# Memory attention's scores as two products of fp32r parts, and a readiness of its own for each pair of heads

## The chip, the core and the metric

The kernel runs on one NeuronCore of a Trainium2 chip. The metric is the device time of one execution in microseconds (us), as the median of several runs. The engines are named as the profile names them: PE is TensorE (PEld is its weight load), DVE is VectorE, ACT is ScalarE, POOL is GpSimd and SP issues the loads from HBM. Each engine works through its own queue in order and waits on semaphores that the others raise.

## What is computed

The program is a small transformer: two layers with differential and forgetting attention over 528 tokens, then a second block over 512 tokens: a gated feed-forward, sparse and stick-breaking attention, cross attention to a memory of 256 tokens, and a last feed-forward. The change touches the cross attention alone:

```python
MEM_HEADS, HEAD_DIM, MEM_LEN = 4, 64, 256

def memory_cross_attention(h, mem_n, wq, wk, wv, wo, g_q, g_k):
    q = rms_norm((h @ wq).reshape(B, T, MEM_HEADS, HEAD_DIM), g_q)      # T = 512
    k = rms_norm((mem_n @ wk).reshape(B, M, MEM_HEADS, HEAD_DIM), g_k)  # M = 256
    v = (mem_n @ wv).reshape(B, M, MEM_HEADS, HEAD_DIM)
    s = jnp.einsum('bqhd,bkhd->bhqk', q, k).astype(jnp.float32) * HEAD_DIM ** -0.5
    p = jax.nn.softmax(s, axis=-1)
    o = jnp.einsum('bhqk,bkhd->bqhd', p, v).reshape(B, T, MEM_HEADS * HEAD_DIM)
    return o @ wo
```

## The kernel before

Activations lie transposed: features on the 128 partitions, tokens along the free dimension. A projection multiplies a weight chunk of 128x1024 with the activations, and both are kept as an fp32r high part and an fp32r low part; three products of parts stand for one product in fp32 (`mm3`, lines 470 to 472). For every weight chunk ACT makes the high part (line 446, `split_hi`) and POOL the low part (line 454, `split_lo`) in the order of the chunks.

The memory stage is written out engine by engine in `memory_pe`, `memory_act`, `memory_dve` and `memory_pool`; the order of each engine's work is the order of these lines, nothing is scheduled at run time. Its parts:

- "mk" 0 and 1 are the keys of the memory, "mq" 0 and 1 the queries, each a tile of 128 features: two heads of 64 features, on partitions 0 to 63 and 64 to 127. "mv" are the values, in two halves of the contraction, and "mo" the output projection. `wout2` is the projection of the stage before.
- A tile of keys or queries goes through `head_out_dve` (line 2149: PSUM times the norm's scale, into `xb`), `head_square_act` (line 2156), `head_norm_pe` (line 2162: mean of squares by a product), `head_norm_act` (lines 2168 and 2170: Ln and Exp) and `head_norm_dve` (line 2182: `xb` times gain and scale, in place).
- Then DVE copies the result for the scores: keys to `KM` (line 2869), queries to `QM` (line 2879). `QM` has one slot of 128 partitions for each of the 4 heads. A head fills 64 of its slot's partitions, the other 64 hold zeros, which a memset at the start of the stage writes (line 2845), so that a product over 128 partitions with `KM`, where both heads of a tile lie, gives one head's scores.
- The scores are 16 units (4 blocks of 128 queries by 4 heads): one fp32 product of 128x128 by 128x256 each. All wait for the copies of all four tiles: `ready=[(v_out, ("mk", 1, "put")), (v_out, ("mq", 1, "put"))]`.

`attention_pe`, `attention_act` and `attention_dve` walk through the units in steps. In step s PE transposes the probabilities of unit s-1 (line 1082), makes the scores of unit s+2 (line 1066), and multiplies the transposed probabilities of unit s-2 with the values (line 1097); three units are scored ahead of the first transposes. DVE takes the maximum of a unit's scores (line 1143), ACT the exponential with its sum (line 1122), and ACT or DVE copies the transposes out of PSUM (lines 1130 and 1159). DVE's first maximum stands behind the last copy to `QM` in its queue. The output projection follows (`mo_cols`).

`xb_read` guards a buffer: "mq" 1 goes to the same half of `xb` in which the keys lie, so it waits until they have been copied.

The sparse attention (`nsa_plan`, earlier in the program) already scores with fp32r parts. Its copies to high parts (line 2227, ACT) and subtractions to low parts (line 2219, DVE) write to `QN` and `KSW`.

Of the kernel before, what the change touches and what calls it, by code (L numbers as in the profile page):

```python
# [8 lines left out]
F32 = mybir.dt.float32  # L9
# [7 lines left out]
T = 512  # L17
# [134 lines left out]
def program(nc, wstream, wpairs, xT, memT, pos, const, param, out):  # L152
# [5 lines left out]
    with ctx:  # L158
# [128 lines left out]
        ml = sb("ml", [128, KT, 256], F32R, at=mem)  # L287
        KM = sb("KM", [128, 2, 256], at=mem)
        VM = sb("VM", [128, 2, 256], at=mem)
        QM = sb("QM", [128, 4, T], at=mem)  # L290
        Pb3 = sb("Pb3", [128, 4, L], at=mem)
# [1834 lines left out]
        def xb_read(on, key):  # L2126

            if key == ("mq", 1):
                on.wait_ge(*v_out["mk", 1, "put"])
            elif key in NORMED[2:]:  # L2130
                was = NORMED[NORMED.index(key) - 2]
                on.wait_ge(*roped[was + ("cos",)])
                on.wait_ge(*rot[was])
# [619 lines left out]
        def memory_pe(e, on):  # L2753
# [41 lines left out]
            for m in range(3, KT):  # L2795
                claim(on, pair(("mo", m), SINGLES), 1, v_out["mo", m])
                mo_cols(m, 0, T, 3).then_inc(*(rows("mo", m) if m % 4 < 3 else tile("mo", m // 4)))

        def mo_done(m):
            return rows["mo", m] if m % 4 < 3 else tile["mo", m // 4]  # L2800

        def memory_act(e, on):
# [18 lines left out]
            head_norm_act(e, on, ("mk", 0))  # L2821
            head_norm_act(e, on, ("mk", 1))
            split_hi(e, on, PART["mq", 1] + 2)
            head_norm_act(e, on, ("mq", 0))
            head_square_act(e, on, ("mq", 1), [sums["memx", 0, 0]])
            split_hi(e, on, PART["mv", 0, 0] + 2)
            head_norm_act(e, on, ("mq", 1))
            for i in range(2):
                on.wait_ge(*token_done("mv", 0, i, 2))
                on.wait_ge(*v_one["rt", "memkv"])  # L2830
                e.activation(VM[:, i, :], token_out("mv", 0, i, 256), ACT.Copy, scale=rTm[:, i:i + 1]).then_inc(
                    *a_out("mv", 0, i))
# [10 lines left out]
        def memory_dve(e, on):  # L2843
            on.wait_ge(*pv["sb", 7])
            e.memset(QM[:, :, :], 0.0).then_inc(*v_one("qm"))
            for c in range(KT):
# [19 lines left out]
            for c in range(2):  # L2866
                head_norm_dve(e, on, ("mk", c))
                on.wait_ge(*x_norm["mk", c])
                e.tensor_copy(KM[:, c, :], head_cols(("mk", c))[1]).then_inc(*v_out("mk", c, "put"))
            head_out_dve(e, on, ("mq", 1), rst[:, 0:T])  # L2870
            for c in range(2):
                head_norm_dve(e, on, ("mq", c))
                if c == 0:
                    turned_scale_dve(e, on, "memkv", 2, rTm)
                on.wait_ge(*x_norm["mq", c])
                on.wait_ge(*v_one["qm"])
                src = head_cols(("mq", c))[1]
                for j in range(2):
                    r = e.tensor_copy(QM[64 * j:64 * j + 64, 2 * c + j, :], src[64 * j:64 * j + 64, :])
                r.then_inc(*v_out("mq", c, "put"))  # L2880
            attention_dve(e, on, plans["mem"])
# [18 lines left out]
        def mem_plan():  # L2900
            units = []
            for i in range(4):
# [3 lines left out]
                for m in range(4):  # L2906
                    u = len(units)
                    units.append(Unit(
                        terms=[(QM[:, m, c0:c0 + 128], KM[:, m // 2, :], 0, 256, True, True)], n=256, o0=0,
                        banks=(u % 3, 1), ready=[(v_out, ("mk", 1, "put")), (v_out, ("mq", 1, "put"))],  # L2910
                        total=(rs[:, i % 2, m:m + 1], [(v_end, ("mem", i - 2, "recip"))] if i >= 2 else []), group=key,
# [350 lines left out]
```

## Time and profile before

| | before |
|---|---|
| median of 3 runs | 1870.87 us (1869.71 to 1872.06) |
| the profiled execution's own time | 1871.18 us |
| its span in the trace | 1869.4 us |
| granted TensorE clock, mean over the span | 0.999 of full speed |
| PE busy | 1831.7 us (98%) |
| DVE, ACT, POOL busy | 1152.4, 770.4, 466.5 us |

The trace shows for each instruction when it started on its engine, how long it took, and, where the engine stood idle ahead of it, for how long and what ended that. PE's matmuls are pipelined: neighbours overlap in the trace, so the distance between starts is their price, not the duration. Times in the rows are microseconds from the start of the span. The memory stage's keys, queries and values lie at about 1449 to 1477 us, its attention at 1477 to 1496 us.

### The profile page before, as it was taken

The page shows a single profiled execution, that of the slowest core. Times are in us where ns is not written, and L with a number is a line of the kernel's source. Part 1 is how long each engine was busy: PE and PEld are TensorE (multiplying, and loading weights), DVE is VectorE, ACT ScalarE, POOL GpSimd, SP SyncE. Part 2 cuts the span into 40 slices and gives each one's busy share as a digit, 9 for nine tenths or more (in the row PEclk, how much of TensorE's full clock was granted, in tenths as well). Part 3 has the DMA queues.
Part 4 walks back from the last instruction along what each step waited for, and adds up shares of the span by engine and source line. Part 5 has one row for each costly group of instructions (what it writes and reads, how often), then busy time and mean ns, then how long its engine had stood idle before and what let it go on. Part 6 is the DMA issues. An engine that isn't in the chain of part 4 may idle for free.

```text
span 1869.4 us, 29612 instructions
## 1 busy us (share of the span) xinstructions
PE 1831.7 (98%) x12020; PEld 1631.1 (87%) x12020; DVE 1152.4 (62%) x1677; ACT 770.4 (41%) x1392; POOL 466.5 (25%) x322
## 2 busy tenths in 40 slices
PE   8999999999999999999999999999999999999999
PEld 8999888979988887899988877989768878999887
DVE  7533465555416657999984555646556579999631
ACT  4122455311235644444433324445564644444331
POOL 5443211354341122000034423320003420000343
PEclk9999999999999999999999999999999999999999
DMA  4322000222220012432322223200003213323132
GB/s 165 97 84 91 35 12 13 80 90 103 80 90 2 23 46 80 140 109 91 102 74 94 98 102 126 86 24 1 1 1 120 84 57 126 115 99 103 69 100 102
DMA packets 41048, 145.49 MB, mean 78 GB/s; under 512 B 5072, under 2 KB 5328, under 8 KB 40784
## 3 DMA queue, kind: packets, MB, share of 16 engines
q1 hardware_dynamic: 40912, 143.59, 22.5%
q8 instruction: 96, 1.57, 0.3%
q14 instruction: 40, 0.33, 0.1%
HBM read 140.40 MB, written 2.10 MB: 76 GB/s over the span
## 4 chain that ended last, share of the span: by engine, by line
PE 87%; DVE 7%; ACT 3%; issue 2%; DMA 1%; POOL 0%; SPq 0%; DVEq 0%; ACTq 0%
PE ps L470 22%; PE ps L471 22%; PE ps L472 22%; PE ps L1066 6%; PE ps L1097 5%; PE ps L1082 2%; PE ps L2675 1%; PE ps L2658 1%; ACT wh L446 1%; DVE xl L560 1%; DVE XSl L1691 1%; PE ps L2416 1%; PE ps L2646 1%; PE ps L1276 1%; DMA raw<-wstream 1%
## 5 line engine op out<-in xcount | busy, mean ns | idle before, releaser
L454 POOL TENSOR_TENSOR wl<-raw,wh 128x1024 fp32r<-128x1024 f32 (+1 forms) x170 | 411.7, 2422 | 1032.8 <-ACT wh L446 1032.7
L446 ACT ACTIVATE wh<-raw 128x1024 fp32r<-128x1024 f32 (+1 forms) x178 | 188.5, 1060 | 604.7 <-PE ps L472 533.1
L470 PE MATMUL ps<-xh,wh 128*128 128x264 f32 (+3 forms) x1144 | 384.4, 336 | 9.5 <-DVE wl L466 3.4
L471 PE MATMUL ps<-xl,wh 128*128 128x264 f32 (+3 forms) x1144 | 380.8, 333 | 0.0
L472 PE MATMUL ps<-xh,wl 128*128 128x264 f32 (+3 forms) x1144 | 380.3, 332 | 0.0
L470 PE MATMUL ps<-XSh,wh 128*128 128x256 f32 (+1 forms) x864 | 284.2, 329 | 5.7 <-DVE wl L1749 3.7
L471 PE MATMUL ps<-XSl,wh 128*128 128x256 f32 (+1 forms) x864 | 284.1, 329 | 0.0
L472 PE MATMUL ps<-XSh,wl 128*128 128x256 f32 (+1 forms) x864 | 283.6, 328 | 0.0
L470 PEld LDWEIGHTS ps<-xh,wh 128*128 128x128 f32 x1144 | 215.2, 188 | 37.6 <-issue 7.3
L471 PEld LDWEIGHTS ps<-xl,wh 128*128 128x128 f32 x1144 | 215.3, 188 | 22.4 <-issue 1.0
L472 PEld LDWEIGHTS ps<-xh,wl 128*128 128x128 f32 x1144 | 215.4, 188 | 21.9
L470 PEld LDWEIGHTS ps<-XSh,wh 128*128 128x128 f32 x864 | 162.7, 188 | 23.5 <-issue 4.9
L472 PEld LDWEIGHTS ps<-XSh,wl 128*128 128x128 f32 x864 | 163.3, 189 | 15.9
L471 PEld LDWEIGHTS ps<-XSl,wh 128*128 128x128 f32 x864 | 162.8, 188 | 16.1
L470 PE MATMUL ps<-XSh,whx 128*128 128x256 f32 x496 | 139.9, 282 | 0.0
L471 PE MATMUL ps<-XSl,whx 128*128 128x256 f32 x496 | 139.7, 282 | 0.0
L472 PE MATMUL ps<-XSh,wlx 128*128 128x256 f32 x496 | 139.2, 281 | 0.0
L1143 DVE TENSOR_REDUCE nm<-ps 128x1 f32<-128x144 f32 (+7 forms) x208 | 100.0, 490 | 55.6 <-PE ps L1066 55.3
L470 PE MATMUL ps<-wh,xh 128*128 128x256 f32 (+1 forms) x352 | 100.6, 286 | 0.3 <-DVE xb L2149 0.3
L471 PE MATMUL ps<-wl,xh 128*128 128x256 f32 (+1 forms) x352 | 99.3, 282 | 0.0
L472 PE MATMUL ps<-wh,xl 128*128 128x256 f32 (+1 forms) x352 | 99.3, 282 | 0.0
L472 PEld LDWEIGHTS ps<-XSh,wlx 128*128 128x128 f32 x496 | 93.9, 189 | 0.0
(419 smaller groups left out, 3470.1 us busy)
## 6 DMA issues: line engine op xcount, KB each, us to landing
raw<-wstream SPq DMA_DIRECT2D x176, 512.0 KB, 3.3
rawx<-wpairs SPq DMA_DIRECT2D x44, 512.0 KB, 3.5
raw<-wpairs SPq DMA_DIRECT2D x24, 512.0 KB, 3.5
raw<-wstream SPq DMA_DIRECT2D x10, 528.0 KB, 3.4
h<-xT SPq DMA_DIRECT2D x4, 528.0 KB, 6.2
out<-h SPq DMA_DIRECT2D x8, 256.0 KB, 4.3
xs<-wpairs SPq DMA_DIRECT2D x2, 512.0 KB, 4.5
HF<-wpairs SPq DMA_DIRECT2D x2, 512.0 KB, 5.4
```

The costliest lines, as they stand in the source:

```text
L446: e.activation(wh[p % 2][:, 0:n], raw[c % 2][:, 0:n], ACT.Copy).then_inc(*w_hi(p))
L454: e.tensor_tensor(wl[p % 2][:, 0:n], raw[c % 2][:, 0:n], wh[p % 2][:, 0:n].bitcast(F32), ALU.subtract).then_inc(*w_lo(p))
L470: e.matmul(o, w_h, x_h, start=start, stop=False)
L471: e.matmul(o, w_h, x_l, start=False, stop=False)
L472: return e.matmul(o, w_l, x_h, start=False, stop=stop)
L560: e.scalar_tensor_tensor(dl, src, gain, dh.bitcast(F32), ALU.mult, ALU.subtract).then_inc(*v_lo(st, k))
L1066: r = e.matmul(ps[:, x.o0 + lo:x.o0 + hi], lhsT, rhs, start=start, stop=stop)
L1082: r = e.transpose(ps[0:b - a, 128 * j:128 * j + 128], plan.source(u)[:, a:b], ident)
L1097: r = e.matmul(PS[:, lo + x.cols[0]:lo + x.cols[1]], buf[0:b - a, 128 * j:128 * j + 128], x.value(j, b - a), start=j == 0 and (x.first or ...
L1143: e.tensor_reduce(nm[:, u % 8:u % 8 + 1], PS[:, lo:lo + x.n], AX.X, ALU.max, negate=True).then_inc(*peak(name, u))
L1276: r = e.transpose(ps[:, 128 * j:128 * j + nq], src[:, 128 * j:128 * j + 128], ident[0:nq, 0:nq])
L1691: e.tensor_tensor(mixed_rows(XSl, i), MIXED[i], mixed_rows(XSh, i).bitcast(F32), ALU.subtract).then_inc(*v_lo(st, "x", i))
```

## The change

`QM`, `KM` and a new `KML` hold fp32r. `QM` of a head now holds the query's high part on the head's own 64 partitions and its low part on the other 64; no zeros are left, and the memset goes. `KM` has a slot for each head, with the key's high part on both halves of the partitions; `KML` holds the key's low part once. A unit's scores are two products: `QM` by `KM` over 128 partitions (high by high and low by high), and the query's high half by `KML` over 64 partitions (high by low).

The high parts are made by ACT (`memory_high_act`: four copies of 64x256 for a key tile, two of 64x512 for a query tile), the low parts by DVE (`memory_low_dve`: two subtractions for a tile), which waits for ACT's. They replace DVE's copies. Units 0 and 1 wait for the parts of the keys and of "mq" 0, units 2 and 3 for those of "mq" 1.

```diff
-        KM = sb("KM", [128, 2, 256], at=mem)
+        KM = sb("KM", [128, 4, 256], F32R, at=mem)
+        KML = sb("KML", [128, 2, 256], F32R, at=mem)
-        QM = sb("QM", [128, 4, T], at=mem)
+        QM = sb("QM", [128, 4, T], F32R, at=mem)
...
             if key == ("mq", 1):
-                on.wait_ge(*v_out["mk", 1, "put"])
+                on.wait_ge(*v_lo["mk", 1])
...
+        def memory_high_act(e, on, key):
+
+            kind, c = key
+            on.wait_ge(*x_norm[key])
+            for j, (p0, p1) in enumerate(((0, 64), (64, 128))):
+                src = head_cols(key)[1][p0:p1]
+                if kind == "mq":
+                    r = e.activation(QM[p0:p1, 2 * c + j, :], src, ACT.Copy)
+                else:
+                    e.activation(KM[p0:p1, 2 * c + j, :], src, ACT.Copy)
+                    r = e.activation(KM[64 - p0:128 - p0, 2 * c + j, :], src, ACT.Copy)
+            r.then_inc(*a_out(*key, "high"))
+
+        def memory_low_dve(e, on, key):
+            kind, c = key
+            on.wait_ge(*x_norm[key])
+            on.wait_ge(*a_out[key + ("high",)])
+            for j, (p0, p1) in enumerate(((0, 64), (64, 128))):
+                src = head_cols(key)[1][p0:p1]
+                if kind == "mq":
+                    dst, high = QM[64 - p0:128 - p0, 2 * c + j, :], QM[p0:p1, 2 * c + j, :]
+                else:
+                    dst, high = KML[p0:p1, c, :], KM[p0:p1, 2 * c + j, :]
+                r = e.tensor_tensor(dst, src, high.bitcast(F32), ALU.subtract)
+            r.then_inc(*v_lo(*key))
...
             head_norm_act(e, on, ("mk", 0))
             head_norm_act(e, on, ("mk", 1))
+            for c in range(2):
+                memory_high_act(e, on, ("mk", c))
             split_hi(e, on, PART["mq", 1] + 2)
             head_norm_act(e, on, ("mq", 0))
             head_square_act(e, on, ("mq", 1), [sums["memx", 0, 0]])
+            memory_high_act(e, on, ("mq", 0))
             split_hi(e, on, PART["mv", 0, 0] + 2)
             head_norm_act(e, on, ("mq", 1))
+            memory_high_act(e, on, ("mq", 1))
...
-            on.wait_ge(*pv["sb", 7])
-            e.memset(QM[:, :, :], 0.0).then_inc(*v_one("qm"))
...
             for c in range(2):
                 head_norm_dve(e, on, ("mk", c))
-                on.wait_ge(*x_norm["mk", c])
-                e.tensor_copy(KM[:, c, :], head_cols(("mk", c))[1]).then_inc(*v_out("mk", c, "put"))
+            for c in range(2):
+                memory_low_dve(e, on, ("mk", c))
             head_out_dve(e, on, ("mq", 1), rst[:, 0:T])
             for c in range(2):
                 head_norm_dve(e, on, ("mq", c))
                 if c == 0:
                     turned_scale_dve(e, on, "memkv", 2, rTm)
-                on.wait_ge(*x_norm["mq", c])
-                on.wait_ge(*v_one["qm"])
-                src = head_cols(("mq", c))[1]
-                for j in range(2):
-                    r = e.tensor_copy(QM[64 * j:64 * j + 64, 2 * c + j, :], src[64 * j:64 * j + 64, :])
-                r.then_inc(*v_out("mq", c, "put"))
+                memory_low_dve(e, on, ("mq", c))
...
-                        terms=[(QM[:, m, c0:c0 + 128], KM[:, m // 2, :], 0, 256, True, True)], n=256, o0=0,
-                        banks=(u % 3, 1), ready=[(v_out, ("mk", 1, "put")), (v_out, ("mq", 1, "put"))],
+                        terms=[(QM[:, m, c0:c0 + 128], KM[:, m, :], 0, 256, True, False),
+                               (QM[p0:p0 + 64, m, c0:c0 + 128], KML[p0:p0 + 64, m // 2, :], 0, 256, False, True)],
+                        n=256, o0=0, banks=(u % 3, 1),
+                        ready=[(v_lo, ("mk", 1)), (a_out, ("mq", m // 2, "high")), (v_lo, ("mq", m // 2))],
```

ACT's queue in the memory stage, before, from the Exp of "mk" 1 (line 2170, 128x256) to the split of the last chunk ahead of the attention:

```order
L2170 ACTIVATE scratch<-scratch 128x256 [waits s_a_one]
L446 ACTIVATE wh<-raw 128x1024 [waits s_tile,d_raw1]
L2168 ACTIVATE scratch<-ps 128x512 [waits s_sums]
L2170 ACTIVATE scratch<-scratch 128x512 [waits s_a_one]
L2156 ACTIVATE scratch<-xb 128x512 [waits s_v_out]
L446 ACTIVATE wh<-raw 128x1024 [waits s_tile,d_raw0]
L2168 ACTIVATE scratch<-ps 128x512 [waits s_sums]
L2170 ACTIVATE scratch<-scratch 128x512 [waits s_a_one]
L2831 ACTIVATE VM<-ps,small 128x256 [waits s_v_one,s_rows]
L2831 ACTIVATE VM<-ps,small 128x256 [waits s_tile]
L446 ACTIVATE wh<-raw 128x1024 [waits d_raw1]
```

The same queue of the change from its last copy of the keys on (seven more copies to `KM` stand ahead of the first row here; lines are one to 31 higher):

```order
L2810 ACTIVATE KM<-xb 64x256
L447 ACTIVATE wh<-raw 128x1024 [waits s_tile,d_raw1]
L2169 ACTIVATE scratch<-ps 128x512 [waits s_sums]
L2171 ACTIVATE scratch<-scratch 128x512 [waits s_a_one]
L2157 ACTIVATE scratch<-xb 128x512 [waits s_v_out]
L2807 ACTIVATE QM<-xb 64x512 [waits s_x_norm]
L2807 ACTIVATE QM<-xb 64x512
L447 ACTIVATE wh<-raw 128x1024 [waits s_tile,d_raw0]
L2169 ACTIVATE scratch<-ps 128x512 [waits s_sums]
L2171 ACTIVATE scratch<-scratch 128x512 [waits s_a_one]
L2807 ACTIVATE QM<-xb 64x512 [waits s_x_norm]
L2807 ACTIVATE QM<-xb 64x512
```

The eight copies of the keys stand ahead of the split of the second half of the values' chunk, the first two of the queries ahead of the split of "mo" 0, the last two ahead of the copies to `VM` and of the last split; each group waits for a result of DVE (`s_x_norm`).

DVE's queue before, from the norm of "mk" 1 to the first maxima:

```order
L2182 SCALAR_TENSOR_TENSOR xb<-xb,par,scratch 128x256 [waits s_a_one]
L2869 COPY KM<-xb 128x256 [waits s_x_norm]
L2149 TENSOR_TENSOR xb<-ps,rst 128x512 [waits s_v_out,s_tile]
L2182 SCALAR_TENSOR_TENSOR xb<-xb,small,scratch 128x512 [waits s_a_one]
L573 TENSOR_SCALAR small<-ps 128x2 [waits s_one_mm]
L2879 COPY QM<-xb 64x512 [waits s_v_one,s_x_norm]
L2879 COPY QM<-xb 64x512
L2182 SCALAR_TENSOR_TENSOR xb<-xb,small,scratch 128x512 [waits s_a_one]
L2879 COPY QM<-xb 64x512 [waits s_x_norm]
L2879 COPY QM<-xb 64x512
L1143 TENSOR_REDUCE nm<-ps 128x1 [waits s_score] x5
```

And of the change, from the low parts of "mk" 0 on:

```order
L2823 TENSOR_TENSOR KML<-xb,KM 64x256 [waits s_a_out,s_x_norm]
L2823 TENSOR_TENSOR KML<-xb,KM 64x256
L2823 TENSOR_TENSOR KML<-xb,KM 64x256 [waits s_a_out,s_x_norm]
L2823 TENSOR_TENSOR KML<-xb,KM 64x256
L2150 TENSOR_TENSOR xb<-ps,rst 128x512 [waits s_v_lo,s_tile]
L2183 SCALAR_TENSOR_TENSOR xb<-xb,small,scratch 128x512 [waits s_a_one]
L574 TENSOR_SCALAR small<-ps 128x2 [waits s_one_mm]
L2823 TENSOR_TENSOR QM<-xb,QM 64x512 [waits s_a_out,s_x_norm]
L2823 TENSOR_TENSOR QM<-xb,QM 64x512
L2183 SCALAR_TENSOR_TENSOR xb<-xb,small,scratch 128x512 [waits s_a_one]
L2823 TENSOR_TENSOR QM<-xb,QM 64x512 [waits s_a_out,s_x_norm]
L2823 TENSOR_TENSOR QM<-xb,QM 64x512
```

DVE's copies became subtractions that wait for ACT (`s_a_out`); the maxima (now line 1144) still stand behind the last of them.

PE's queue at the first units, before:

```order
L1066 MATMUL ps<-KM,QM 128x256 [waits s_v_out]
L1066 MATMUL ps<-KM,QM 128x256 [waits s_a_one]
L1066 MATMUL ps<-KM,QM 128x256 [waits s_a_out]
L1082 MATMUL ps<-identR,Pb 128x128 [waits s_prob,s_a_out]
L1082 MATMUL ps<-identR,Pb 128x128
```

and of the change:

```order
L1067 MATMUL ps<-KM,QM 128x256 [waits s_a_out,s_v_lo,s_v_out]
L1067 MATMUL ps<-KML,QM 128x256
L1067 MATMUL ps<-KM,QM 128x256 [waits s_a_one]
L1067 MATMUL ps<-KML,QM 128x256
L1067 MATMUL ps<-KM,QM 128x256 [waits s_v_lo,s_a_out]
L1067 MATMUL ps<-KML,QM 128x256
L1083 MATMUL ps<-identR,Pb 128x128 [waits s_prob,s_a_out]
```

Each score is two products now, and the third unit has the wait for the parts of "mq" 1 (`s_v_lo`) that the first two are free of.

## Rows read from the trace of the kernel before

**Rows 1.** The page's busy time: us (share of the span) xinstructions

```profile
PE 1831.7 (98%) x12020; PEld 1631.1 (87%) x12020; DVE 1152.4 (62%) x1677; ACT 770.4 (41%) x1392; POOL 466.5 (25%) x322
```

**Rows 2.** Windows: length, PE, PEld, DVE, ACT, POOL busy, PEclk, DMA, GB/s

```profile
1482.00:1492.00 10.00, 10.00 (x79) 9.54 (x78) 6.51 (x19) 7.22 (x28) 1.38 (x2) 1.00 0.13 48
```

**Rows 3.** Timeline of PE, one step of the attention, and the first "mo" product

```profile
1487.83 0.39 PE L1082 MATMUL ps<-identR,Pb 128*128 128x128 f32 x2
1488.06 0.60 PE L1066 MATMUL ps<-KM,QM 128*128 128x256 f32 x2
1488.49 0.55 PE L1097 MATMUL ps<-VM,PT 128*128 128x64 f32 x4
1488.88 0.39 PE L1082 MATMUL ps<-identR,Pb 128*128 128x128 f32 x2
...
1496.36 0.42 PE L470 MATMUL ps<-amh,wh 128*128 128x384 f32 x1
```

**Rows 4.** Groups of instructions by line, 1477 to 1497 us

```profile
L1066 PE MATMUL ps<-KM,QM 128*128 128x256 f32 x32 | 9.3, 383 | 0.9 <-DVE QM L2879 0.9
```

**Rows 5.** Timeline of PE, second half of the values and first scores

```profile
1473.91 0.28 PE L471 MATMUL ps<-wl,mh 128*128 128x256 f32 x1
...
1476.51 0.28 PE L472 MATMUL ps<-wh,ml 128*128 128x256 f32 x1
1477.72 1.53 PE L1066 MATMUL ps<-KM,QM 128*128 128x256 f32 x6 [0.94 <-DVE QM L2879]
1479.60 0.41 PE L1082 MATMUL ps<-identR,Pb 128*128 128x128 f32 x2 [0.34 <-ACT Pb L1122]
```

**Rows 6.** Timeline of DVE, norms, copies to QM, first maxima

```profile
1464.61 1.48 DVE L2182 SCALAR_TENSOR_TENSOR xb<-xb,par,scratch 128x256 f32<-128x256 f32 x1 [1.63 <-ACT scratch L2170]
...
1470.97 1.85 DVE L2182 SCALAR_TENSOR_TENSOR xb<-xb,small,scratch 128x512 f32<-128x512 f32 x1 [1.61 <-ACT scratch L2170]
...
1475.29 1.39 DVE L2182 SCALAR_TENSOR_TENSOR xb<-xb,small,scratch 128x512 f32<-128x512 f32 x1 [1.42 <-ACT scratch L2170]
1476.72 0.86 DVE L2879 COPY QM<-xb 64x512 f32<-64x512 f32 x2
1478.43 1.29 DVE L1143 TENSOR_REDUCE nm<-ps 128x1 f32<-128x256 f32 x3 [0.85 <-PE ps L1066]
```

**Rows 7.** Timeline of ACT and DVE: parts made in other stages

```profile
1186.73 2.58 ACT L2227 ACTIVATE KSW<-scratch 64x512 fp32r<-64x512 f32 x4 [3.12 <-DVE scratch L2211]
...
1188.04 2.79 DVE L2219 TENSOR_TENSOR KSW<-scratch,KSW 64x512 fp32r<-64x512 f32 x4 [1.34 <-ACT KSW L2227]
...
1486.44 0.41 ACT L1312 ACTIVATE amh<-xb 128x256 fp32r<-128x256 f32 x1
```

**Rows 8.** Timeline of ACT between the keys and the attention

```profile
1468.73 1.06 ACT L446 ACTIVATE wh<-raw 128x1024 fp32r<-128x1024 f32 x1 [3.43 <-PE ps L472]
...
1472.46 1.06 ACT L446 ACTIVATE wh<-raw 128x1024 fp32r<-128x1024 f32 x1 [1.01 <-PE ps L472]
1473.99 0.60 ACT L2168 ACTIVATE scratch<-ps 128x512 f32<-128x512 f32 x1 [0.47 <-PE ps L2162]
...
1476.82 0.47 ACT L2831 ACTIVATE VM<-ps,small 128x256 f32<-128x256 f32 x1 [0.94 <-PE ps L472]
1477.19 1.05 ACT L446 ACTIVATE wh<-raw 128x1024 fp32r<-128x1024 f32 x1
```

**Rows 9.** Timeline of POOL: low parts of mv 1 and mo 0

```profile
1469.86 2.41 POOL L454 TENSOR_TENSOR wl<-raw,wh 128x1024 fp32r<-128x1024 f32 x1 [4.05 <-ACT wh L446]
1473.60 2.53 POOL L454 TENSOR_TENSOR wl<-raw,wh 128x1024 fp32r<-128x1024 f32 x1 [1.33 <-ACT wh L446]
```

**Rows 10.** Timeline of PE: its longest idle time in the span

```profile
959.45 0.47 PE L470 MATMUL ps<-XSh,wh 128*128 128x512 f32 x1 [2.00 <-ACT XSh L1886]
```

**Rows 11.** Windows around what followed it, columns as in the second group

```profile
960.75:961.00 0.25, 0.25 (x2) 0.25 (x1) 0.25 (x1) 0.00 (x0) 0.25 (x1) 0.50 1.02 246
...
964.00:964.25 0.25, 0.25 (x2) 0.16 (x1) 0.25 (x1) 0.00 (x0) 0.00 (x0) 0.79 1.21 492
```

More of the change, by code:

```diff
@@ L2906, in mem_plan @@
                 for m in range(4):
-                    u = len(units)
+                    u, p0 = len(units), 64 * (m % 2)
                     units.append(Unit(
-                        terms=[(QM[:, m, c0:c0 + 128], KM[:, m // 2, :], 0, 256, True, True)], n=256, o0=0,
-                        banks=(u % 3, 1), ready=[(v_out, ("mk", 1, "put")), (v_out, ("mq", 1, "put"))],
+                        terms=[(QM[:, m, c0:c0 + 128], KM[:, m, :], 0, 256, True, False),
+                               (QM[p0:p0 + 64, m, c0:c0 + 128], KML[p0:p0 + 64, m // 2, :], 0, 256, False, True)],
+                        n=256, o0=0, banks=(u % 3, 1),
+                        ready=[(v_lo, ("mk", 1)), (a_out, ("mq", m // 2, "high")), (v_lo, ("mq", m // 2))],
                         total=(rs[:, i % 2, m:m + 1], [(v_end, ("mem", i - 2, "recip"))] if i >= 2 else []), group=key,
```

## The prediction

> **What bounds the kernel now.** I read the page first: PE is busy 98% of the span [rows 1], so only PE's work or PE's waits count. Then the windows of the memory attention: over ten microseconds PE is busy all ten, ACT 7.22 and DVE 6.51 [rows 2]; the steady part is PE's. The timeline of PE gives one step: from transposes to transposes 1.05 us, of which the scores take 0.43, from their start to that of the products with the values [rows 3]. The group by line shows the 16 scores as 32 records, two for each fp32 product [rows 4]. At the head of the stage it is otherwise: the values' products end, PE waits 0.94 us for DVE's last copy to `QM`, scores three units, and waits again 0.34 us for the first exponential [rows 5]. DVE had the norm of "mq" 1, then the two copies, then the maxima [rows 6]. So the stage has two parts with two bounds: a chain ACT, DVE, PE up to the first transposes at 1479.60, and PE from there to the first "mo" product at 1496.36 [rows 3, 5].
>
> **The scores.** An fp32r product of 128x256 costs PE what the values' products show: 22 distances between 1473.91 and 1476.51, 0.118 us each [rows 5]. Two make 0.236 against 0.43: 0.194 saved. The product over 64 partitions has no row. It streams the same 256 columns, so I take the same price; bounds are nothing, and the 0.315 that would leave no gain. Three units are scored ahead of the first transposes, so 13 lie on the PE part: 13 x 0.194 = 2.5 us saved. Of the whole 16 it would be 3.1. A step becomes 0.86 us. ACT's and DVE's shares, 0.72 and 0.65 of a step of 1.05 [rows 2], are 0.76 and 0.68 us, both below 0.86, so PE stays the bound; ACT's margin is thin.
>
> **The memset** stood where DVE waited for the first tile of the output projection. Nobody waits for it: zero gain; had anyone, it would show as a wait for DVE there.
>
> **The parts.** This is the chain that decides, so it is followed instruction by instruction.
>
> Prices: four copies 64x512 to fp32r on ACT took 2.58 us, 0.645 each with no overlap; four subtractions on DVE 2.79, 0.70 each [rows 7]. For 64x256 no row exists. A copy of 128x256 to fp32r took 0.41 [rows 7]; with no overlap I take 0.43, between 0.32 (half of the long one) and 0.645. The subtraction of 64x256 I take at 0.43 too, between 0.35 and 0.70.
>
> A second thing is read from the rows: DVE's norm is held while POOL makes a low part. POOL ran 1469.86 to 1472.27 and 1473.60 to 1476.13 [rows 9]; the norms that began inside these ended at 1472.82 and 1476.68 [rows 6], both 0.55 us behind POOL's end.
>
> 1. The norm of "mk" 0 ends at 1466.09 [rows 6]. ACT's eight copies: 8 x 0.43 = 3.45, to 1469.6. DVE's low parts of "mk" 1 end at 1470.5; only then may "mq" 1 enter `xb`.
> 2. The split queued behind them ran at 1468.73 [rows 8]; now 1469.6 to 1470.65. POOL's part, 2.41 [rows 9], ends at 1473.1. PE's second half of the values was under way at 1473.91 [rows 5], its first product half a microsecond ahead: just not late. This is the cover that hides the eight copies.
> 3. Ln and Exp of "mq" 0 follow the split; from Ln to the norm's start it is 1.30 us (1473.99 to 1475.29 [rows 6, 8]). So DVE could begin at 1471.9, is held by POOL until 1473.1, and ends at 1473.65. ACT's two copies: 1.27, to 1474.95.
> 4. Behind them waits the split of "mo" 0, 1472.46 before [rows 8]: now 1474.95 to 1476.0. Behind that Ln of "mq" 1, 1473.99 before [rows 8]: now 1475.95. DVE could begin the norm at 1477.25. But POOL has moved too: its part of "mo" 0 begins at 1476.05, or at 1476.4 if DVE's second subtraction for "mq" 0 (1475.0 to 1476.4) holds it. It ends at 1478.5 to 1478.8, and the norm 0.55 later: 1479.05 to 1479.35.
> 5. ACT's copies of "mq" 1 to 1480.35 to 1480.65, DVE's subtractions (1.4) to 1481.8 to 1482.1. Only here may DVE's first maximum start, though PE scored units 0 and 1 at about 1476.75. From the first maximum to the first transposes it was 1.17 us (1478.43 to 1479.60 [rows 5, 6]): transposes at 1483.0 to 1483.3 instead of 1479.60, **3.5 us later**.
>
> Queued behind ACT's last copies are the two to `VM` and a split, together 2 us [rows 8]: to 1482.4, when the first exponential's maximum arrives too; no addition, at most 0.2. The early score of two units buys nothing, since the maxima stand behind "mq" 1's parts in DVE's queue.
>
> Bounds of the 3.5: with copies of 0.32, step 1 ends at 1468.65, ahead of the split's old time, and all later steps come 0.95 earlier: 2.6; if besides DVE's two subtractions cost no more than its old copies (0.86 [rows 6]), 2.0. With copies of 0.645 step 1 ends at 1471.25 and all after it is 1.65 later, PE's values too: 5.2.
>
> For these copies the Trainium skill has a price: "ScalarE: Activation LUTs", section "What ACT_TABLE_LOAD costs", gives an ACTIVATE with immediate operands as 186 ns plus 0.833 ns an element and lets back-to-back ones overlap by some 93 ns. That makes 0.31 us for each of the eight and would put the sum 0.9 us lower. This trace does not show the overlap in the nearest case: four copies took four times the duration. The row decides, and the overlap is a rival below.
>
> **The clock.** Between its second score (to 1477.2) and the third (from 1481.8) PE is idle for 4.6 us, and mostly idle to 1483. The longest idle time in the trace is 2.00 us, up to 959.45 [rows 10]. PE then worked, and 1.3 us later the granted clock was down: 0.50 (1.2 GHz) from 960.75 on, and back to full (2.4 GHz) inside the quarter that begins at 964.00 (0.79) [rows 11]: about 3.4 us. A longer gap should do it as well. PE at half clock does half its work, 1.7 us lost if it has work throughout; part of the stretch may fall in the gap, where it is free. I take 1.6, bounds 0 and 3.4 (a second stretch).
>
> **Sum.** 3.5 - 2.5 + 1.6 = +2.6 us. On the profiled execution (1871.18 us, span 1869.4) it gives 1873.8 and a span of 1872.0; that execution lies 0.3 above the median, so on the median of 1870.87 it is 1873.5.
>
> **The rivals.**
> - *Overlapping copies.* Starting 2.6 us later, with the same clock loss: +1.7, 1872.6. For it: ACT's instructions of different lines do overlap, by 0.10 where the split follows the copy to `VM` [rows 8]. Against: the four copies in [rows 7]. The skill's rule above is this one.
> - *The clock holds.* +1.0, 1871.9. For it: the span's mean clock is full but for that one place. Against: the gap is over twice that one's.
> - *The clock stays low for a second stretch.* The first stretch falls in the gap, nothing raises the clock, and the attention runs all of the next at 1.2 GHz, or part of two: +4.3, 1875.2. Against: in [rows 11] one stretch ended it; there PE worked without a pause, here it starts with waits. A sentence of the skill points this way ("TensorE: Matmul & The Clock Gate", Part 4): transposes do not count as work for the clock. No row here tests it.
> - *No gain from the second product.* If the 64-row product costs 0.315 or ACT's margin is used up by waits, the 2.5 us are gone: +5.1, 1876.0. Against: PE's price follows the columns in [rows 3, 5], and both products stream 256.
> - *Faster.* All parts of "mq" 1 are ready when the values end. Then the 16 scores save 3.1 and some 0.4 of PE's old waits goes: -3.5, 1867.4. It decides only if DVE's norm is not held by POOL and ACT's copies of the queries cost under 0.4 each; [rows 6, 7, 9] speak against both.
>
> **How the numbers follow.** Forecast 0.48; overlapping copies 0.12; clock holds 0.15; clock low twice 0.12; no gain 0.08; faster 0.05. 0.2% is 3.7 us, about what a measurement of this kernel can tell from no change. Above it lie "no gain", most of "low twice" and the upper end of the forecast (0.03): slower 0.22. Below it lies the best end of "faster": 0.03. The rest, 0.75, is within. The range is 1870.0 to 1876.2: from the held clock with a start 2.0 late (1870.4) less the scatter of a median of three runs, to "no gain" with a little scatter; it leaves out "faster" and tails.
>
> **What the profile after would show.** The scores as 32 records of 128x256 with a step of 0.86 us at full clock; unit 2's scores waiting about 4.6 us for DVE's line 2823; first transposes at 1483 +- 0.4 (from the span's start, if the stages ahead are equal); norm of "mq" 1 ending 0.55 us behind POOL's part of "mo" 0; a stretch with granted clock 0.50 beginning between 1479 and 1483; values not late. The first "mo" product at about 1499.0. The prediction fails if ACT's short copies cost far from 0.43, if the step does not shrink to 0.86, or if the clock does other than once down for 3.4 us.

## The result, and the profile after

| | before | after |
|---|---|---|
| median | 1870.78 us (1869.71 to 1872.06, 4 runs) | 1892.52 us (1891.83 to 1894.17, 4 runs) |
| the profiled execution, and its span | 1871.18, 1869.4 us | 1891.83, 1890.0 us |
| granted clock, mean over the span | 0.999 | 0.990 |

The ratio is 1.0117, with a 95% interval of 1.0100 to 1.0135: the change costs 21.7 us. The forecast was 1873.5 in a range up to 1876.2, and gave 0.75 to a change too small to measure. The measured time lies 19 us above the forecast and 16 above the range.

The page of after, busy time and the row of the clock; the first line answers to [rows 1]:

```profile
PE 1848.9 (98%) x12020; PEld 1643.8 (87%) x12020; DVE 1153.9 (61%) x1678; ACT 776.4 (41%) x1404; POOL 466.6 (25%) x322
PEclk9999999999999999999999999999999699999999
```

PE's share is 98% in both kernels, and it is no help. The digit 6 in the row of the clock is the first sign: one slice of 47 us in which the granted clock averaged six tenths. Windows of after around it (length, PE, PEld, DVE, ACT, POOL busy, PEclk, DMA, GB/s):

```profile
1480.00:1481.00 1.00, 0.00 (x0) 0.00 (x0) 0.99 (x2) 1.00 (x3) 0.00 (x0) 0.99 0.84 324
1481.00:1482.00 1.00, 0.59 (x2) 0.40 (x2) 0.93 (x3) 0.95 (x2) 0.34 (x1) 0.50 0.10 33
1482.00:1492.00 10.00, 10.00 (x35) 7.54 (x35) 2.73 (x7) 4.58 (x18) 2.01 (x1) 0.50 0.16 54
1492.00:1506.00 14.00, 14.00 (x54) 11.31 (x53) 4.93 (x14) 5.01 (x17) 0.90 (x2) 0.50 0.00 0
...
1518.00:1519.00 1.00, 1.00 (x7) 1.00 (x6) 0.42 (x1) 0.08 (x1) 0.00 (x0) 0.74 0.00 0
1519.00:1520.00 1.00, 1.00 (x8) 1.00 (x7) 0.00 (x0) 0.34 (x1) 0.58 (x1) 1.00 0.00 0
```

The clock went to 1.2 GHz at 1481 and came back at 1518.5, 37.5 us later, while PE's records leave no gap from 1481.41 on. In the ten microseconds from 1482 PE works off 35 products and transposes where before it did 79 [rows 2].

PE's timeline of after, which answers to [rows 3, 5]: the first scores, the wait, one step, and the first "mo" product.

```profile
1475.78 0.28 PE L473 MATMUL ps<-wh,ml 128*128 128x256 f32 x1
1475.90 0.30 PE L1067 MATMUL ps<-KM,QM 128*128 128x256 f32 x1
1476.13 0.38 PE L1067 MATMUL ps<-KML,QM 64*128 64x256 f32 x1
1476.45 0.38 PE L1067 MATMUL ps<-KM,QM 128*128 128x256 f32 x1
1476.76 0.38 PE L1067 MATMUL ps<-KML,QM 64*128 64x256 f32 x1
1481.41 0.55 PE L1067 MATMUL ps<-KM,QM 128*128 128x256 f32 x1 [4.27 <-DVE QM L2823]
...
1482.40 0.69 PE L1083 MATMUL ps<-identR,Pb 128*128 128x128 f32 x2
...
1497.38 0.63 PE L1083 MATMUL ps<-identR,Pb 128*128 128x128 f32 x2
1497.67 0.56 PE L1067 MATMUL ps<-KM,QM 128*128 128x256 f32 x1
1498.16 0.58 PE L1067 MATMUL ps<-KML,QM 64*128 64x256 f32 x1
1498.67 1.11 PE L1098 MATMUL ps<-VM,PT 128*128 128x64 f32 x4
1499.57 0.64 PE L1083 MATMUL ps<-identR,Pb 128*128 128x128 f32 x2
...
1515.73 0.67 PE L471 MATMUL ps<-amh,wh 128*128 128x384 f32 x1
```

Stages ahead put the memory stage 0.7 us earlier in this trace than in that of before, so distances are read from the values' last product. From it to the first transposes it is 6.62 us (3.09 before): 3.53 later, as forecast. From there to the first "mo" product it is 33.33 us (16.76 before), where the forecast said 14.3 plus 1.6. A step is 2.19 us, not 0.86. The excess has two causes. First, the first four products, still at full clock, stand 0.23, 0.32 and 0.31 us apart (1475.90, 1476.13, 1476.45, 1476.76), not 0.118. Their weight loads show why, PEld of after:

```profile
1475.66 0.19 PEld L473 LDWEIGHTS ps<-wh,ml 128*128 128x128 f32 x1
1475.82 0.19 PEld L1067 LDWEIGHTS ps<-KM,QM 128*128 128x128 f32 x1
1476.13 0.18 PEld L1067 LDWEIGHTS ps<-KML,QM 64*128 64x128 f32 x1
1476.45 0.19 PEld L1067 LDWEIGHTS ps<-KM,QM 128*128 128x128 f32 x1
```

Among the values' products a load starts 0.12 us ahead of the product it serves. Between products of 128 and of 64 rows it starts only with that product (1476.13 in both views). Second, the clock: it takes the rest.

The chain of the parts came out as followed on paper. DVE and POOL of after (answering to [rows 6, 9]), and ACT's copies, the first and the last of the keys', and those of the queries (to [rows 8]):

```profile
1476.48 2.00 DVE L2183 SCALAR_TENSOR_TENSOR xb<-xb,small,scratch 128x512 f32<-128x512 f32 x1 [0.78 <-ACT scratch L2171]
1479.88 1.38 DVE L2823 TENSOR_TENSOR QM<-xb,QM 64x512 fp32r<-64x512 f32 x2 [1.40 <-ACT QM L2807]
```

```profile
1475.38 2.55 POOL L455 TENSOR_TENSOR wl<-raw,wh 128x1024 fp32r<-128x1024 f32 x1 [3.02 <-ACT wh L447]
```

```profile
1465.40 0.42 ACT L2809 ACTIVATE KM<-xb 64x256 fp32r<-64x256 f32 x1 [0.83 <-DVE xb L2183]
...
1468.40 0.41 ACT L2810 ACTIVATE KM<-xb 64x256 fp32r<-64x256 f32 x1
...
1478.51 1.27 ACT L2807 ACTIVATE QM<-xb 64x512 fp32r<-64x512 f32 x2 [2.07 <-DVE xb L2183]
```

The copies stand 0.43 us apart (3.00 over seven distances), the norm of "mq" 1 ends at 1478.48, 0.55 behind POOL's 1477.93, and the last subtraction at 1481.26; unit 2 starts 0.15 later.

### The profile page after: what moved, and what is told of

The parts are those of the page before. It is cut to its first block, busy times and chain, and to the rows that moved or that the text cites. A ratio compares the mean times of both kernels' runs of the same rounds, so it can differ in the third digit from the quotient of the medians.

```text
span 1890.0 us, 29629 instructions
## 1 busy us (share of the span) xinstructions
PE 1848.9 (98%) x12020; PEld 1643.8 (87%) x12020; DVE 1153.9 (61%) x1678; ACT 776.4 (41%) x1404; POOL 466.6 (25%) x322
## 4 chain that ended last, share of the span: by engine, by line
PE 85%; DVE 7%; ACT 3%; issue 2%; DMA 1%; POOL 1%; SPq 0%; DVEq 0%; ACTq 0%
PE ps L471 22%; PE ps L473 21%; PE ps L472 21%; PE ps L1067 6%; PE ps L1098 6%; PE ps L1083 3%; ACT wh L447 1%; DMA raw<-wstream 1%; PE ps L2676 1%; PE ps L2659 1%; DVE xl L561 1%; DVE XSl L1692 1%; PE ps L1277 1%; PE ps L2647 1%; PE ps L2417 1%
## 5 line engine op out<-in xcount | busy, mean ns | idle before, releaser
L472 PEld LDWEIGHTS ps<-XSl,whx 128*128 128x128 f32 x496 | 93.9, 189 | 0.0
```

What stands on the lines that cost most here:

```text
L472: e.matmul(o, w_h, x_l, start=False, stop=False)
```

## The experiments

Theory: the loss has three terms, the late start, a dear 64-row product and the clock, and the clock stays down because the stream that follows never raises it. Rivals: the gap alone would do it, whatever follows; or the 64-row product is dear by itself. The table has, for each kernel, the distance from the values' last product to the first transposes ("head"), from there to the first "mo" product ("attention"), both from its trace, the median, and the ratio to the kernel before with its 95% interval (before: 1870.78 of 4 runs for after, 1871.01 of 17 for E1 to E4, 1871.41 of 28 for E5 to E8, 1871.29 of 21 for the rest).

| | head | attention | median, runs | ratio |
|---|---|---|---|---|
| before | 3.09 | 16.76 | | |
| after | 6.62 | 33.33 | 1892.52, 4 | 1.0117 (1.0100 to 1.0135) |
| E1, 128-row low product | 6.56 | 17.10 | 1874.72, 10 | 1.0023 (1.0008 to 1.0037) |
| E2, after, gap filled late | 10.92 | 19.26 | 1882.35, 4 | 1.0059 (1.0044 to 1.0074) |
| E3, E1, gap filled late | 10.61 | 14.30 | 1876.60, 7 | 1.0028 (1.0017 to 1.0039) |
| E4, before with a longer gap | 9.59 | 17.72 | 1878.83, 5 | 1.0041 (1.0027 to 1.0055) |
| E5, after, gap kept busy | 6.61 | 19.23 | 1877.20, 5 | 1.0032 (1.0019 to 1.0044) |
| E6, E1, gap kept busy | 6.61 | 14.34 | 1872.35, 10 | 1.0004 (0.9995 to 1.0013) |
| E7, E1, early maxima | 3.99 | 15.81 | 1873.09, 11 | 1.0010 (1.0001 to 1.0019) |
| E8, E7, gap kept busy | 3.96 | 15.80 | 1871.61, 11 | 1.0003 (0.9994 to 1.0012) |
| E9, after, burst midway | 6.57 | 28.06 | 1887.18, 4 | 1.0085 (1.0071 to 1.0099) |
| E10, E5, low product twice | 6.74 | 20.78 | 1879.55, 4 | 1.0045 (1.0029 to 1.0060) |
| E11, before, readiness alone | 2.34 | 16.77 | 1870.06, 11 | 0.9993 (0.9984 to 1.0001) |
| E12, E8, splits moved | 4.88 | 14.55 | 1871.53, 11 | 1.0000 (0.9992 to 1.0009) |

### E1: the low product over 128 rows

```diff
-KML = sb("KML", [128, 2, 256], F32R, at=mem)
+KML = sb("KML", [128, 4, 256], F32R, at=mem)
...
+e.memset(KML[:, :, :].bitcast(F32), 0.0).then_inc(*v_one("kml"))
...
-(QM[p0:p0 + 64, m, c0:c0 + 128], KML[p0:p0 + 64, m // 2, :], 0, 256, False, True)
+(QM[:, m, c0:c0 + 128], KML[:, m, :], 0, 256, False, True)
```

> The second product of a score runs over all 128 partitions: KML has a slot for each head, the low part in the head's own half, zeros in the other (a memset of KML, early in the stage); QM's low half meets the zeros, so the scores are the same. Everything else is as in the changed kernel, the wait of 4.3 us ahead of the third unit too. Theory: the product over 64 partitions is what costs (0.31 us for each product at full clock, because neither weight load overlaps the other product's streaming), and it is also what keeps the clock down for the whole attention. Then the two products cost 0.236 us at full clock, the clock falls at 1481 and is back after one or two stretches of 3.4 us, and the time is 1873 to 1875. Rival: the long wait alone lowers the clock and no attention of this kind raises it again, whatever its products. Then the step at half clock is about 1.65 us, the clock is down until the output projection, and the time is about 1884.

The low part lies in the head's own half of its slot, and DVE writes zeros to the other early in the stage. It measured 1874.72, within what was expected. The 16 products that it changes stream the same 256 columns as before, and 17.8 us come back. Windows of E1, columns as above:

```profile
1482.00:1484.00 2.00, 2.00 (x12) 2.00 (x11) 0.85 (x2) 1.83 (x7) 1.10 (x1) 0.50 0.00 0
...
1486.00:1488.00 2.00, 2.00 (x14) 2.00 (x13) 0.60 (x2) 1.07 (x4) 0.00 (x0) 0.60 0.02 6
1488.00:1490.00 2.00, 2.00 (x21) 2.00 (x20) 1.54 (x5) 1.35 (x7) 0.00 (x0) 1.00 0.03 8
```

The gap is as long (PE waits 4.85 us here for the same subtraction), the clock falls too (1480.75), but it is back before 1488, some 7 us later. So in these two kernels the clock falls in the gap, and what follows makes the difference in how long it stays down.

One of the ten runs took 1886.76 us. No trace of it was taken, but its granted clock is on record: 0.988 in the mean, against 0.997 or 0.998 in the other nine and 0.990 in after. By that mean it spent some 45 us at half clock (an estimate: 0.012 of its 1885 us, doubled). Where is open; the time fits a clock that stayed down through the attention here too (the rival above had 1884). So with 128-row products the clock was low only briefly in nine runs of ten, and it isn't shown that it always comes back.

### E2 and E3: idle products in the gap, put too late

18 products of 128x512 whose results nobody uses, on after and on E1.

```diff
 ps = claim(on, *x.banks, prob[plan.name, u])
+if plan.name == "mem" and u == 2:
+    spare = claim(on, 7, 1)
+    for _ in range(18):
+        e.matmul(spare, identR[:, :], xmh[:, 0, :], start=True, stop=True)
```

> The changed kernel, with 18 idle products of 128x128 by 128x512 (about 4.2 us) on PE between the second unit's scores and the wait for the parts of mq 1; they write to a PSUM bank that nobody reads. Theory: the clock falls because of the wait, so it now stays full; each pair of products costs 0.63 instead of 0.43 us, 13 of them 2.6 us; with the start 3.5 us late the time is 1877. Rival: the mixed stream of products over 128 and 64 partitions lowers the clock by itself. Then the clock falls soon after the attention begins and the time is 1888 to 1892.

> Both edits: second product over 128 partitions and 18 idle products in the wait. Theory: no clock loss, step 0.86 us, the start 3.5 us late: +1.0, 1872. Rival (ACT's and DVE's work binds the step once PE's is below it): step 0.95 to 1.05, the 2.5 us are not gained, 1873.5 to 1874.4.

Both numbers are missed, by a fault of mine: the products stood behind a claim of a bank that waits for ACT's copies to `VM`. In E3 they began only after 3.77 us of idle time, and lengthened the head by 4 us. PE's timeline of E3:

```profile
1480.01 5.99 PE L1067 MATMUL ps<-xmh,identR 128*128 128x512 f32 x18 [3.77 <-ACT VM L2866]
```

One thing can be read all the same. In E2 the clock fell all the same (1483.75), some 3.5 us later it was back to full, while the idle products still ran, and the attention behind them, 64-row products and all, stayed there and took 19.26 us instead of 33.33.

### E4: the kernel before with the same kind of gap

DVE makes "mq" 1's copies to `QM` five times over, so PE waits 6.62 us.

```diff
+for k in range(8 if c else 0):
+    e.tensor_copy(QM[64 * (k % 2):64 * (k % 2) + 64, 2 + k % 2, :],
+                  src[64 * (k % 2):64 * (k % 2) + 64, :]).then_inc(*v_one("late", k))
+    on.wait_ge(*v_one["late", k])
```

> The kernel before with eight extra copies of the same data to QM's last slots on DVE, 0.42 us each with a wait between them, so that PE waits about 4.3 us longer (0.94 + 3.9 or so) for QM and then scores in fp32. Theory: the wait lowers the clock, and the attention of the kernel before, whose PE work has no products over 64 partitions, raises it again after one or two stretches of 3.4 us: +3.8 for the copies and 1.7 to 3.4 for the clock, 1876 to 1878. Rival: no attention raises a fallen clock: PE at half clock for all 16 units, a step of 2.1 us, +3.8 and +16, about 1890.

Windows of E4:

```profile
1486.00:1488.00 2.00, 2.00 (x11) 1.66 (x11) 0.67 (x2) 1.56 (x6) 0.00 (x0) 0.69 0.00 0
1488.00:1490.00 2.00, 2.00 (x17) 1.90 (x17) 1.17 (x4) 1.21 (x5) 0.00 (x0) 1.00 0.00 0
```

A longer gap than in after, fp32 scores behind it, and the clock is back before 1488, again some 7 us after it fell (1480.4). The rival that the gap alone keeps it down falls. The copies made the head 6.5 us longer where 3.8 was meant, so 1878.83 lies above the 1876 to 1878 expected.

### E5 and E6: the gap kept busy from its start

The same idle products ahead of the claim, 19 on after and 20 on E1.

```diff
+if plan.name == "mem" and u == 2:
+    spare = claim(on, 7, 1)
+    for _ in range(19):
+        e.matmul(spare, identR[:, :], xmh[:, 0, :], start=True, stop=True)
 ps = claim(on, *x.banks, prob[plan.name, u])
```

> The changed kernel (second product over 64 partitions) with 19 idle products of 128x128 by 128x512, now directly behind the second unit's scores and ahead of every wait of the third unit. Theory: the clock stays full, the pair costs 0.63 us where the fp32 product cost 0.43, a step is 1.25 us; with the start 3.5 us late the time is 3.5 + 13 x 0.2 = 6.1 us above before, 1877. Rival: the stream with products over 64 partitions lowers the clock without any wait; then it falls in the attention and the time is 1885 to 1892.

> Second product over 128 partitions (zeros in the other half of KML) and 20 idle products in the same place. Theory: no clock loss and a step of 0.86 us: 3.5 - 2.5, so 1.0 above before, 1872, and 2 to 3 below the same kernel without the idle products. Rival: the clock was not what the 3.9 us of the kernel without idle products came from, but a start later than 3.5 us: then the idle products change nothing and the time is 1874.7.

Both came in on the number. E5 is after without the clock: 1877.2, so the clock's share is 15.3 us. Its step, and then that of E6, which differs in the low product alone (PE; the lines are shifted by four):

```profile
1486.75 0.66 PE L1102 MATMUL ps<-VM,PT 128*128 128x64 f32 x4
1487.24 0.39 PE L1087 MATMUL ps<-identR,Pb 128*128 128x128 f32 x2
1487.39 0.36 PE L1071 MATMUL ps<-KM,QM 128*128 128x256 f32 x1
1487.68 0.38 PE L1071 MATMUL ps<-KML,QM 64*128 64x256 f32 x1
1487.99 0.66 PE L1102 MATMUL ps<-VM,PT 128*128 128x64 f32 x4
```

```profile
1488.10 0.38 PE L1087 MATMUL ps<-identR,Pb 128*128 128x128 f32 x2
1488.24 0.36 PE L1071 MATMUL ps<-KM,QM 128*128 128x256 f32 x1
1488.44 0.28 PE L1071 MATMUL ps<-KML,QM 128*128 128x256 f32 x1
1488.55 0.55 PE L1102 MATMUL ps<-VM,PT 128*128 128x64 f32 x4
1488.94 0.39 PE L1087 MATMUL ps<-identR,Pb 128*128 128x128 f32 x2
```

E5's step is 1.24 us (1486.75 to 1487.99), E6's 0.84 (1488.10 to 1488.94). From `KM` to `KML` it is 0.29 against 0.20, from `KML` to the values 0.31 against 0.11, and the values' group takes 0.50 against 0.39: 0.40 us a step, all of it at and around the two places where the rows change. The loads show the same as in after: in E6 that of `KML` starts 0.12 us ahead of its product, in E5 with it. Over the attention that is 19.23 - 14.34 = 4.9 us.

### E7 and E8: the head shortened

E1, with DVE's maxima of units 0 and 1 ahead of the subtractions of "mq" 1, and ACT's splits of the two "mo" chunks in steps 2 and 5 of the attention; E8 has 11 idle products besides. The comments below say where a line stood or stands; they are not in the code.

```diff
-            split_hi(e, on, PART["mv", 0, 0] + 2)     # ahead of the norm of "mq" 1
...
-            split_hi(e, on, PART["mv", 0, 1] + 2)     # ahead of the attention
+                if name == "mem" and s in (2, 5):
+                    split_hi(e, on, PART["mv", 0, int(s > 2)] + 2)
...
+                    for u in range(2):                # ahead of memory_low_dve of "mq" 1
+                        on.wait_ge(*score["mem", u])
+                        e.tensor_reduce(nm[:, u:u + 1], PS[:, lo:lo + 256], AX.X, ALU.max, negate=True).then_inc(
+                            *peak("mem", u))
```

> Second product over 128 partitions, and the head of the stage in another order: on DVE the maxima of units 0 and 1 stand ahead of the subtractions for mq 1; on ACT the splits of the two chunks of mo stand inside the attention (steps 2 and 5) instead of ahead of mq 1's norm and ahead of the attention. Theory: the norm of mq 1 is no longer held by POOL, the parts of mq 1 are ready 2.2 us earlier, the first transposes come at about the old time, and the 2.5 us of the scores are gained: 1868.5 if the clock holds; the wait of PE is still 2.4 us long, and if the clock falls the gain is 0.8 or less, about 1870. Rival: ACT has no room for the two splits in the attention (1.06 us each): 1 to 2 us lost, 1870 to 1872.

> The same with 11 idle products (about 2.5 us) on PE ahead of the third unit's waits. Theory: the clock holds: 1868.5 to 1869. Rival: the clock had held without them: no difference to the kernel without idle products.

Both numbers are missed: E7 took 1873.09 where 1868.5 to 1870 was expected, and E8 1871.61, some 3 us above its own. The head became 2.65 us shorter than in E6. DVE of E8, the same norm with POOL idle beside it:

```profile
1476.39 0.75 DVE L2190 SCALAR_TENSOR_TENSOR xb<-xb,small,scratch 128x512 f32<-128x512 f32 x1
```

0.75 us instead of 2.00. Still the head is 0.87 us longer than in the kernel before, where the old length was expected. About half of E8's miss is a new wait, of PE for exponentials that ACT makes behind the moved splits, E8 (the second one is 0.39 at 1485.82):

```profile
1482.65 0.44 PE L1087 MATMUL ps<-identR,Pb 128*128 128x128 f32 x2 [0.68 <-ACT Pb L1129]
```

The attention lost 1.46 us by it against E6.

E7 shows something on the clock as well. Its PE waits without anything to do, and the clock holds:

```profile
1481.37 0.36 PE L1067 MATMUL ps<-KM,QM 128*128 128x256 f32 x1 [2.87 <-DVE QM L2826]
```

```profile
1480.00:1482.00 2.00, 0.63 (x5) 0.66 (x6) 1.32 (x3) 1.51 (x6) 0.00 (x0) 1.00 0.00 0
```

So the idle products of E8 changed nothing in the traced attention (15.80 against 15.81), which was E8's rival. Whether the clock held in E7's other runs isn't shown: their mean clocks range from 0.996 to 1.000.

### E9: a burst in the middle

E5's lines with 14 products at `u == 8`, on after.

> The changed kernel with 14 idle products of 128x512 on PE ahead of the scores of unit 8, in the middle of the attention; their results are used by nobody. Theory (the clock is down because the stream with 64-row products at 1.2 GHz never raises it; the same stream leaves a full clock alone): the clock falls near 1481.5 as before, steps are 2.19 us up to unit 8's, the idle products bring the clock to 1.00 within 3 to 4 us, and from there on the steps are 1.25 us to the end. 9.5 steps x 0.95 = 9.0 us saved, 1.4 more because the mo products start at full clock, the idle products cost 4.7: 1886.8. Rival (a stream with 64-row products lowers the clock again whenever it runs a few us): the clock falls back after the burst, steps again 2.19, about 1895 to 1897.

It measured 1887.18. PE and windows of E9:

```profile
1494.93 4.59 PE L1066 MATMUL ps<-xmh,identR 128*128 128x512 f32 x14
```

```profile
1497.00:1498.00 1.00, 1.00 (x5) 0.77 (x5) 0.00 (x0) 0.00 (x0) 0.00 (x0) 0.84 0.00 0
...
1501.00:1510.00 9.00, 9.00 (x61) 7.31 (x61) 4.82 (x15) 6.00 (x22) 1.45 (x2) 1.00 0.00 0
```

Fourteen products without use make the kernel 5.3 us faster than after. The clock was back 2.5 us after the first of them. Up to them the step is 2.19 us, behind them 1.24, to the end. In this trace the same stream leaves either clock as it finds it, for as long as it lasts.

### E10: the low product twice in a row

E5, with each unit's 64-row product issued twice.

> As the changed kernel with the gap kept busy (1877.2, step 1.245, clock full), but each unit's product over 64 partitions is issued twice in a row (high by low is counted twice in the scores). Theory A (the price is that of the change from 128 rows to 64 and back): the second one costs no more than 0.12 us, step 1.36, 13 to 16 x 0.12 = 1.6 to 1.9 us more, about 1879. Theory B (each 64-row product costs 0.31 by itself, since its weight load doesn't overlap): step 1.56, 4.1 to 5.0 us more, about 1882.

1879.55, 2.35 above E5. Its attention is 1.55 longer, and a step 1.36 us, 0.12 more than E5's. PE of E10:

```profile
1488.25 0.39 PE L1087 MATMUL ps<-identR,Pb 128*128 128x128 f32 x2
...
1488.69 0.50 PE L1071 MATMUL ps<-KML,QM 64*128 64x256 f32 x2
1489.12 0.66 PE L1102 MATMUL ps<-VM,PT 128*128 128x64 f32 x4
1489.61 0.39 PE L1087 MATMUL ps<-identR,Pb 128*128 128x128 f32 x2
```

The pair takes 0.43 where one took 0.31. So a 64-row product behind another (here with the same operands) costs 0.12, what a 128-row one does: the price is that of the change of rows, and theory B falls.

### E11: the readiness alone

```diff
-ready=[(v_out, ("mk", 1, "put")), (v_out, ("mq", 1, "put"))]
+ready=[(v_out, ("mk", 1, "put")), (v_out, ("mq", m // 2, "put"))]
```

> The kernel before with the readiness alone: fp32 scores and DVE's copies as they were, units 0 and 1 wait for the keys and mq 0 only. Theory: units 0 and 1 are scored while DVE normalises mq 1, DVE's first maximum follows its last copy without the 0.85 us wait for PE, first transposes 0.7 to 0.8 earlier, no gap over 2 us, clock untouched: 0.8 us under the kernel before. Rival (readiness buys nothing, as the prediction said of the changed kernel, since the maxima stand behind mq 1's copies and ACT's first exponential is held by its split until 1478.2): same as before, 0 to 0.3 us.

The head is 0.75 us shorter (2.34), the attention as before. The time, 1.2 us lower with an interval that reaches 1.0001, does not tell it from before; the trace does.

### E12: the splits elsewhere

E8, with one split ahead of ACT's copies of "mq" 1 and the other in step 10.

> As the kernel with 128-row low products, early maxima and 11 idle products (1871.6, span 1869.2), but the split of mo 0 stands in ACT's queue ahead of the copies of mq 1, where ACT was idle 1.02 us, and the split of mo 1 in step 10 of the attention. Theory (what that kernel lost was PE waiting for exponentials behind the splits, 0.68 + 0.39 us): about 0.7 to 1.0 us faster than it, 1870.7. Rival (POOL's low part of mo 0 now lies beside DVE's subtractions for mq 1 and holds them until 0.55 us behind its end): first transposes some 0.5 to 1 us later, nothing gained, 1871.5 to 1872.5.

1871.53: nothing gained on E8, and both mechanisms were there. The attention is 1.25 us shorter, 14.55. The head is 0.92 longer. DVE and POOL of E12:

```profile
1479.41 2.27 DVE L2830 TENSOR_TENSOR QM<-xb,QM 64x512 fp32r<-64x512 f32 x2 [0.75 <-ACT QM L2814]
```

```profile
1478.05 2.40 POOL L455 TENSOR_TENSOR wl<-raw,wh 128x1024 fp32r<-128x1024 f32 x1 [4.17 <-ACT wh L447]
```

The two subtractions take 2.27 us where they took 1.39 in E8. If the second takes half of that 1.39, the first ends some 0.5 us behind POOL's 1480.45, held as the norms were.

## Why the prediction was wrong

**The start, 3.5 us: right.** 3.53 in after, and 3.5 in E1, E5, E6 and E9, which have the same order (3.65 in E10). The hold by POOL with its 0.55 us and the values not being late were read from rows of before, and held; so did the 0.43 for a short copy, which was chosen between bounds and not read from a row. "Overlapping copies" fell with it: the eight copies show no overlap. Of the hold, the Trainium skill ("SBUF — State Buffer", on the two separate sides of SBUF) says that a DVE instruction with two SBUF inputs and a GpSimd instruction that reads SBUF take a pair of ports in turn, each for its whole length. The traces agree: 2.00 us beside POOL, the last 0.55 of them behind POOL's end, and 0.75 without.

**The scores, -2.5 us: the step that failed first.** "The product over 64 partitions has no row. It streams the same 256 columns, so I take the same price." The saving would have been right for a product over 128 partitions: E6's attention is 16.76 - 14.34 = 2.4 us shorter. That it came out so near is in part luck: the pair takes 0.31 there (0.20 and 0.11) and not 0.236, and the transposes ahead of it 0.14 where they took 0.23 ahead of the fp32 product, which the prediction did not foresee. Over 64 it is 2.5 longer (E5: 19.23), a difference of 4.9 us. The bounds of the prediction were at fault as well. They were made for the one product and ended at 0.315, which is what its distance measured; but the product before it and the group behind it pay too, 0.09 and 0.11 us. The rival "no gain" had the place and not the size. A rule of the Trainium skill stood against this change, and I had not weighed it: "TensorEngine Tiling (Array Packing)", key properties of the tiling modes, says that a change of the tiling mode drains TensorE, while a change of tile inside a mode does not. E5 and E10 agree with it: some 0.2 us at each change, none between two 64-row products.

**The clock, +1.6 us: the step that failed by most.** That it would fall in the gap was right, and from when. "Back to full inside" one stretch of 3.4 us was carried over from another stage [rows 11], where dense 512-column products followed the gap. Here it stayed down for 37.5 us and cost 15.3. The 3.4 us itself was one execution's: PE waits 2.0 to 2.95 us at that place in all 14 traces, and the clock falls behind it in five of them. Even with 128-row products (E1) it was down for about 7 us, which cost 2.4 us of time (1874.72 against 1872.35): the rival "low for a second stretch" is what E1 is. Its page, "TensorE: Matmul & The Clock Gate" of the Trainium skill, Part 4, on transposes not counting as work, does not explain the difference, since E1 and after have the same transposes. None of the rivals let the state last as long as the stream that found it.

**The sum.** Start 3.5, attention at full clock +2.5, clock 15.3: 21.3 of the 21.7 us measured. The clock's term is the difference of two medians, those of after and E5. Without the clock and over 128 rows it is E6: 3.5 - 2.4 = 1.1 by its trace (the prediction had 1.0), 0.9 measured.

**The early readiness** was said to buy nothing, and that was wrong, though the sum made use of it. The forecast let the first maximum start right behind DVE's last subtraction, as it does in after; with the old readiness it would first wait for PE's scores, as in before (0.85 us [rows 6]). On the kernel before, the readiness makes the head 0.75 us shorter (E11). No run takes it out of after.

**Open.** What in the stream with 64-row products fails to raise the clock: in what PE runs, these products are the only difference from E1, but no run tells the changes of rows from the products themselves. What the run of E1 with 1886.76 us did is open too. No kernel here was measurably faster than before: E6, E8, E11 and E12 are all within 0.1% of it.

## What to carry to other kernels

Price an instruction by a row of its own shape in its own neighbourhood. A product over half the partitions streams no faster, and set singly among full ones it adds 0.40 us to a step of 0.84 (E5, E6). Fill the other half with zeros, or put several of them in a row (the second of two cost 0.12 in E10). And after any gap on PE that lowers the clock, ask whether the stream behind it can raise it again: if not, the gap is charged to everything up to the next dense stretch. Keeping PE busy across the gap with products of no use is a cheap test of that, and told 15 us here.

## What the hardware showed that was not expected

- The granted clock stayed at 0.50 for 37.5 us with PE's records busy for all but the first 0.4 us. The same instructions ran at 1.00 for 19 us in E5 and for the last 13 us ahead of "mo" in E9.
- Between products over 128 and over 64 partitions the weight load starts with its product (after, E5); between equal ones it starts 0.12 us ahead (the values' products in after, `KML` in E6).
- The same idle time doesn't lower the clock each time. In waits of PE of 3.19 to 6.62 us ahead of the attention, or right behind them, it fell in all six traces that have one (after, E1 to E4, E9); behind the 2.87 us of E7 it did not, and behind the 1.99 to 2.95 us near 959 it did in five traces of 14 (before, E8, E9, E10, E12). It fell also where PE hardly waited: near 217.3 in the traces of E2 and E7, for some 6.7 us, with no idle time over 0.62 us in the 17 us ahead of it.
- DVE's subtractions are held beside POOL's as its norms are: 2.27 us for two against 1.39 (E12, E8).
